# A hybrid attention and convolution layer: channel tiles reordered, the last two run by token halves, output weights split earlier

## The reference, cut to what matters

```
h    = rms_norm(x)
q, kv, gates, z_a, ch, cb, cc, cz = split(h @ w_in)
o_a  = (g0*compressed + g1*selected + g2*window attention) * silu(z_a)   # 8 heads x 64
u    = cc * ch
o_b  = cb * (conv3(u) + conv_b) * silu(cz)                               # 512 channels
out  = x + concat(o_a, o_b) @ w_out
```

## Time and profile before

| | us |
|---|---|
| median of three runs (lowest, highest) | 678.46 (677.49, 678.79) |
| the profiled execution's own time | 678.36 |
| its span, first to last instruction | 676.6 |
| TensorE busy | 654.6 (97%) |
| VectorE busy | 484.9 (72%) |
| ScalarE busy | 379.5 (56%) |
| GpSimd busy | 197.0 (29%) |

### The profile page before, as it was taken

The page is one execution under the profiler, slowest core; times in us unless marked ns, Lnnn a source line. Parts: engine busy times, 40 slices in busy tenths (PEclk is TensorE's granted clock), DMA queues, the critical chain, the costliest instruction groups (busy, mean ns, idle before and its releaser), DMA issues.

```text
span 676.6 us, 10300 instructions
## 1 busy us (share of the span) xinstructions
PE 654.6 (97%) x3513; PEld 550.9 (81%) x3513; DVE 484.9 (72%) x1151; ACT 379.5 (56%) x883; POOL 197.0 (29%) x216
## 2 busy tenths in 40 slices
PE   8999999999999999999989999899899999999998
PEld 5889998878887888888777888788678788887776
DVE  4945989984756555776687876878877768777753
ACT  6744458554435354466555674657875556655641
POOL 3423204523423232431222312123842221212120
PEclk9999999999999999999999999999999999999999
DMA  8423202211111111100101101011411001001111
GB/s 316 140 55 111 63 1 63 63 32 47 50 45 32 47 32 32 48 18 30 32 16 32 32 17 31 1 63 55 162 35 60 34 32 63 32 32 38 57 32 63
DMA packets 19636, 36.30 MB, mean 54 GB/s; under 512 B 2816, under 2 KB 4224, under 8 KB 19584
## 3 DMA queue, kind: packets, MB, share of 16 engines
q1 hardware_dynamic: 19440, 35.63, 16.9%
q10 hardware_dynamic: 144, 0.00, 0.0%
HBM read 31.43 MB, written 4.19 MB: 53 GB/s over the span
## 4 chain that ended last, share of the span: by engine, by line
PE 81%; DVE 10%; ACT 4%; issue 4%; DMA 1%; SPq 0%; POOL 0%; ACTq 0%; DVEq 0%
PE pf L1398 10%; PE pf L1399 9%; PE pf L1400 9%; PE tp L1691 7%; PE sc L1536 4%; PE pj L1400 4%; PE pj L1399 4%; PE pj L1398 4%; PE sc L1535 4%; PE po L1671 4%; PE po L1672 4%; PE sc L1398 3%; PE sc L1400 3%; PE sc L1399 3%; DVE ptl L1332 1%
## 5 line engine op out<-in xcount | busy, mean ns | idle before, releaser
L904 ACT CAST pth<-tp 128x512 fp32r<-128x512 f32 (+1 forms) x148 | 86.8, 586 | 119.8 <-PE tp L1691 118.6
L1310 DVE CUSTOM_DVE_ANT_0 sc<-sc,maskb 128x64 f32<-128x64 f32 (+8 forms) x192 | 103.2, 561 | 49.9 <-PE sc L1536 49.3
L1332 DVE TENSOR_TENSOR ptl<-tp,pth 128x512 fp32r<-128x512 f32 x132 | 91.1, 690 | 39.1 <-ACT pth L904 38.5
L627 POOL TENSOR_SCALAR qp<-qp,precip,gate 128x64 f32<-128x64 f32 x64 | 44.4, 694 | 175.4 <-DVE precip L1300 175.2
L1691 PE MATMUL tp<-cst,qp 128*128 128x128 f32 (+1 forms) x592 | 88.9, 272 | 2.4 <-issue 1.3
L1398 PE MATMUL pf<-hh,fh 128*128 128x512 f32 x200 | 80.6, 403 | 2.7 <-DVE mixc L1269 1.9
L1691 PEld LDWEIGHTS tp<-cst,qp 128*128 128x128 f32 (+1 forms) x592 | 68.8, 137 | 12.3 <-issue 3.4
L1399 PE MATMUL pf<-hl,fh 128*128 128x512 f32 x200 | 78.3, 392 | 0.0
L1400 PE MATMUL pf<-hh,fl 128*128 128x512 f32 x200 | 78.2, 391 | 0.0
L587 POOL TENSOR_TENSOR fl<-fraw,fh 128x512 fp32r<-128x512 f32 x36 | 48.7, 1354 | 92.7 <-ACT fh L753 92.7
L578 POOL TENSOR_TENSOR wl<-qp,wh 128x512 fp32r<-128x512 f32 (+1 forms) x33 | 49.3, 1519 | 88.8 <-ACT wh L667 85.2
(11 more groups left out here) (243 smaller groups left out, 1548.5 us busy)
## 6 DMA issues: line engine op xcount, KB each, us to landing
fraw<-in_wside SPq DMA_DIRECT2D x36, 256.0 KB, 2.6
qp<-in_wpack SPq DMA_DIRECT2D x28, 256.0 KB, 3.1
wor<-in_wout SPq DMA_DIRECT2D x16, 256.0 KB, 2.8
xo<-in_x SPq DMA_DIRECT2D x16, 256.0 KB, 2.8
out<-xo SPq DMA_DIRECT2D x16, 256.0 KB, 2.1
mixc<-in_xcm SPq DMA_DIRECT2D x4, 512.0 KB, 7.2
xlow<-in_xcm SPq DMA_DIRECT2D x3, 512.0 KB, 6.4
qp<-in_wpack SPq DMA_DIRECT2D x5, 224.0 KB, 2.6
```

The costliest lines, as they stand in the source:

```text
L904: nc.scalar.copy(pth[ptn % 2][0:r, :], tp[tpn % 2][0:r, :]).then_inc(pth_ready, 1)
L1310: return V.tensor_tensor_reduce(row, row, mask, -1.0, -NEG, ALU.add, ALU.min, most)
L1332: V.tensor_tensor(ptl[ptn % 2][:, :], tp[tpn % 2][:, :], pth[ptn % 2][:, :].bitcast(F32), ALU.subtract).then_inc(tp_read, 1)
```

## The change

1. In each group of four channel tiles cz now comes before cb. `cz_done` becomes `cz_used`: cb waits for the cz product, and cz, not cb, waits for the end of the convolution in its second half.
2. The last two tiles, cz3 and cb3, run by token halves: cz3 first half, cb3 first half, cz3 second half, cb3 second half. Their weights are loaded and split once for each half: `NHALF`, the count of loads of 256 KB, goes from 36 to 40.
3. The ACT operation that begins a convolution (L877) leaves the side work of step c (13, 29, 50, 74) and stands in step c+1 behind the exponentials and the first probability copy. On DVE the first convolution piece goes to the end of its step, and the others behind the side work of the first group.
4. The output weights are split in steps 81 to 84 (first eight pieces) and 87 to 90 (last eight) instead of 84 to 91. Four raw pieces of the first eight wait in `wor` or, for two of each four, in `xo`.
5. `xo`, `msh`, `msl` get memory of their own. The first `mixc` split goes from step 86 to 83, and the first `mixn` split from 88 to 85.
6. `SIDE` has no (0, 0) and no (1, 1) step any more. Three output halves (0, 1 and 13 of 0 to 15) run as four steps of (2, 0) each.
7. In the front, `keys_hi(0, 4, 1)` and `keys_lo(0, 4, 1)` go ahead of two z items; on DVE also ahead of the normalisation of the compressed key.

```diff
-    TILES += [("ch", t, 1816 + P * t), ("cc", t, 2840 + P * t), ("cb", t, 2328 + P * t), ("cz", t, 3352 + P * t)]
+    TILES += [("ch", t, 1816 + P * t), ("cc", t, 2840 + P * t), ("cz", t, 3352 + P * t), ("cb", t, 2328 + P * t)]
-NHALF = 2 * NTILES
+RUNS = [(n, hf) for n in range(NTILES - 2) for hf in range(2)]
+RUNS += [(n, hf) for hf in range(2) for n in (NTILES - 2, NTILES - 1)]
+SHARED = 2 * (NTILES - 2)
+NHALF = SHARED + 2 * (NF - SHARED)
+def first_load(f):
+    return 2 * (f // 2) if f < SHARED else 2 * f - SHARED
+def last_user(h):
+    return h // 2 * 2 + 1 if h < SHARED else (h + SHARED) // 2
+def load_source(h):
+    return h if h < SHARED else 2 * RUNS[last_user(h)][0] + h % 2
...
-SIDE = [(2, 2)] * 36 + [(2, 1), (2, 1), (2, 0)] * 17 + [(0, 0)] + [(1, 1)] * 8
-SIDE += [(2, 1), (2, 1), (2, 0)] * ((NS - len(SIDE)) // 3 + 2)
-SIDE = SIDE[:NS + 6] + [(4, 0)] * 4
+LONG = (NF, NF + 1, NX - 3)
+SIDE = [(2, 2)] * 36
+for x in range((SIDE_FIRST + sum(map(sum, SIDE))) // 8, NX - 2):
+    SIDE += [(2, 0)] * 4 if x in LONG else [(2, 1), (2, 1), (2, 0)]
+SIDE += [(4, 0)] * 4
...
-        if step_of(OUT_0 + 16 * m - (5 if m else 1)) == k:
+        if step_of(OUT_0 + 16 * m - (5 if m else 9)) == k:
...
-        if step_of(OUT_0 + 16 * m) == k:
+        if step_of(OUT_0 + 16 * m - (0 if m else 3)) == k:
...
-WOUT_STEP = step_of(OUT_0 - 9) + 1
+WOUT_STEPS = step_of(OUT_0 - 17) + 1, step_of(OUT_0 - 1) + 1
...
 # SP
-            for j in range(NK):
+            for j in range(NK + 4):
                 output_weights(j)
-            sp.wait_ge(f_done, NF)
+            sp.wait_ge(wol_ready, NK)
             for c in range(2):
                 residual(c)
...
 # ACT, front
             root(S_CK, 1, HD, ck_std)
+            keys_hi(0, 4, 1)
             item(E_Z, 1)
             item(E_Z, 2)
-            keys_hi(0, 4, 1)
             hidden(1)
...
 # ACT, side(f)
-                elif kind == "cc" and f % 2 == 1:
-                    bank_free(act, f - 1)
-                    bank_free(act, f)
-                    A(mixc[:, t, :], ub[:, 2:2 + SEQ], ACT.Identity, ...)
+            def convolve_first(t):
+                f = 2 * CONV_TILES[t] + 1
+                bank_free(act, f - 1)
+                bank_free(act, f)
+                A(mixc[:, t, :], ub[:, 2:2 + SEQ], ACT.Identity, ...)
...
 # ACT, step k, behind the exponentials and the first prob_hi
+                if k - 1 in CONV_STEPS:
+                    convolve_first(CONV_STEPS.index(k - 1))
...
-                    act.wait_ge(f_done, NF - 1 if j < NK else NF)
-                    nc.scalar.copy(woh[:, kt, cols], wor[j % 4][:, :]).then_inc(woh_ready, 1)
+                    act.wait_ge(f_done, NF - 2 if j < NK else NF)
+                    nc.scalar.copy(woh[:, kt, cols], weight_rows(j)[:, :]).then_inc(woh_ready, 1)
...
 # DVE, front
             V.tensor_reduce(stat[:, 0, S_CK:S_CK + 1], cksq[:, :], AX.X, ALU.add).then_inc(ck_sum, 1)
+            keys_lo(0, 4, 1)
             inv_std(S_CK, 1, HD, ck_std, 1)
...
             item(E_Z, 2)
-            keys_lo(0, 4, 1)
...
 # DVE, step k
-                for t, j in conv_pieces_at(k):
-                    convolve(t, j)
                 for f in side_ends(k, 0):
                     if f < NF:
                         side(f)
                 for c in out_ends(k, 0):
                     residual(c)
+                for t, j in conv_pieces_at(k):
+                    if j:
+                        convolve(t, j)
...
                 for c in out_ends(k, 1):
                     residual(c)
+                for t, j in conv_pieces_at(k):
+                    if j == 0:
+                        convolve(t, j)
```

More of the change, by code:

```diff
@@ L226, in mixn_half_at @@
     for m in range(LAST):
-        if step_of(OUT_0 + 16 * m) == k:
+        if step_of(OUT_0 + 16 * m - (0 if m else 3)) == k:
             return m
     return None
-CONV_STEPS = [step_of(16 * n + 15) for n in range(NTILES) if TILES[n][0] == "cc"]
+CONV_TILES = [n for n in range(NTILES) if TILES[n][0] == "cc"]
+CONV_STEPS = [step_of(16 * n + 15) for n in CONV_TILES]
 def conv_pieces_at(k):
@@ L241 @@
     for hf in range(2):
-        assert step_of(16 * TILES.index(("cb", t, 2328 + P * t)) + 8 * hf + 7) >= c + 2 + 2 * hf
-WOUT_STEP = step_of(OUT_0 - 9) + 1
+        assert step_of(8 * RUNS.index((TILES.index(("cz", t, 3352 + P * t)), hf)) + 7) >= c + 2 + 2 * hf
+WOUT_STEPS = step_of(OUT_0 - 17) + 1, step_of(OUT_0 - 1) + 1
 LAST_STEPS = (output_step(2 * LAST) + 6, output_step(2 * LAST + 1))
 def wout_at(k):
-    return [j for j in range(2 * NK) if WOUT_STEP + j // 2 == k]
+    return [NK * n + j for n in range(2) for j in range(NK) if WOUT_STEPS[n] + j // 2 == k]
 def wout_piece(j):
@@ L333, in hybrid_layer @@
                     fl[s] = sb(f"fl{s}", [P, 512], F32R, d)
[L334 to L339, removed]
+                with ExitStack() as f:
+                    fraw = [sb(f"fraw{s}", [P, 512], F32, f) for s in range(2)]
                 wor = [None, None] + [sb(f"wor{s}", [P, 512], F32, d) for s in (2, 3)]
@@ L348, in hybrid_layer @@
                 with ExitStack() as f:
-                    ub = sb("ub", [P, SEQ + 2], F32, f)
-                with ExitStack() as f:
                     wor[0], wor[1] = (sb(f"wor{s}", [P, 512], F32, f) for s in (0, 1))
+                ub = sb("ub", [P, SEQ + 2], F32, d)
+                xo = [sb(f"xo{s}", [P, 512], F32, d) for s in range(2)]
+                msh = sb("msh", [P, NK, P], F32R, d)
+                msl = sb("msl", [P, NK, P], F32R, d)
         with ExitStack() as c:
@@ L489, in half_free, with weight_rows @@
             else:
-                eng.wait_ge(f_done, h - 2)
+                eng.wait_ge(f_done, last_user(h - 3) + 1)
+        def weight_rows(j):
+            return xo[j % 4 - 2] if j < NK and j % 4 >= 2 else wor[j % 4]
         block = ctx.enter_context(nc.Block())
@@ L860, in side @@
             def side(f):
-                kind, t, _ = TILES[f // 2]
-                cols = slice(f % 2 * 512, (f % 2 + 1) * 512)
+                n, hf = RUNS[f]
+                kind, t, _ = TILES[n]
+                cols = slice(hf * 512, (hf + 1) * 512)
                 if kind in ("z", "cz"):
                     act.wait_ge(f_done, f + 1)
-                    if kind == "cz" and 2 * t + f % 2:
-                        act.wait_ge(cz_done, 2 * t + f % 2)
+                    if kind == "cz" and 2 * t + hf:
+                        act.wait_ge(cz_used, 2 * t + hf)
                     if kind == "z" and f >= 1:
@@ L1576, in channels @@
                 ins = three(side_bank(f), fh[h % 3][:, c], fl[h % 3][:, c], hh[:, k, s], hl[:, k, s], k == 0, k == NK - 1)
-                if hf == 1 and k == 3:
+                if k == 3 and last_user(h) == f:
                     ins.then_inc(half_used, 1)
```

49 lines of the change are left out of this document (24 added, 25 removed).

## The result

| | before | changed |
|---|---|---|
| median of four runs, us | 678.1 | 668.97 |
| lowest and highest | 677.49, 678.79 | 668.78, 669.98 |
| profiled execution, us | 678.36 | 669.98 |
| its span | 676.6 | 668.2 |

The ratio is 0.9868, with a 95% interval of 0.9851 to 0.9885: 1.3% faster. The predicted time was 670.8 us. The kernel before has one run more here than ahead of the change (677.73). The profiled execution of the changed kernel is the slowest of its four, so the two spans lie 8.4 us apart and the medians 9.1. Of the difference 0.7 us is found in the traces: from about 11 us on TensorE stands 0.7 us later in this execution, because its first operands came later; the last matmul of the hidden layer's first part starts at 149.17 us, before at 148.47.

A forecast was written before the change was run, and what follows sets the result against it. TensorE, 97% busy with unchanged matrix work, was the bound, so only its waits could go: 0.8 + 1.4 + 3.9 + 2.9 + 0.6 - 1.4 - 0.6 = 7.6 us, from 678.36 to 670.8. Likeliest range 669 to 673, wide range 667.0 to 677.0.

The forecast's parts named there:

- The front: Before the channels: the transposes' 1.38 us wait for DVE goes, the first channel split comes later; gain 0.8 us.
- L877 behind the exponentials: Waits behind ACT's first convolution operation go: 1.4 us in steps 14 and 30, 3.1 in steps 51 to 53 and 75.
- The bank after an attention output: Steps 54 and 78: a channel half's wait for DVE shortens by 0.74 us each, together 1.5.
- DVE's load as a discount: Steps 51 to 78: with DVE 96% busy some wait comes back, so of 4.6 us gain 3.9 is taken.
- Rival A: VectorE is the bound behind the waits: steps 51 to 78 gain 1.5, 86 to 94 gain 1.7; 675.0 us, chance 0.25.
- Steps 86 to 88 and 92 to 94: Waits of turn, scores and flush go in 86 to 88, gain 2.9 us; two like flushes in 92 to 94, 0.6.
- Four more splits: Extra channel splits in steps 78 to 82 slow DVE; with second cz operations and shifted residuals, loss 1.4 us.
- the weights split sooner: Output weights split from step 81: the 6.7 us buffer chain just fits two steps of some 3.6 us; taken at nothing.
- B: Rival: slower, as ACT waits for output weights in steps 81 to 84 and 87 to 90; 682.0 us, chance 0.07.
- The end: Steps 128 to 131: a second turn followed at once by its flush, afterwards also in step 131; loss 0.6 us.

The follow-up runs named there:

- keys_old: Changed kernel with the key copies of the front back in their old order on ACT and DVE: 669.94 us.
- conv_old: Changed kernel with ACT's first convolution operation back in the side work, ahead of the next exponentials; DVE's order stays new: 674.2 us.
- before_conv: Kernel before, with only ACT's first convolution operation moved behind the next step's exponentials and DVE's first piece to the end of its step: 672.61 us.
- pieces_first: Changed kernel with DVE's convolution pieces 1 to 3 back ahead of the side work of group 1: 670.11 us.
- swap_back: Changed kernel with cb ahead of cz again in every group of four, and their waits to match: 668.68 us.
- thin_steps: Changed kernel with the old step list: step 87 without a part, steps 88 to 95 with (1, 1): 671.64 us.
- shift_back: Changed kernel with the third output half of four (2, 0) steps being number 2 instead of 13: 669.37 us.

## Why the prediction was right, and where its terms were not

The forecast was 670.8 us, by its likeliest case 669 to 673; the median is 668.97, at that case's edge. The mechanism, waits that go while the matrix work stays, is shown. By its steps:

- **The front**, 0.8: 1.0 by medians in `keys_old`, 0.8 by the traces. It was right also in what is late next, the first channel split.
- **L877 behind the exponentials**, 1.4 and 3.1: shown, each wait with the size read. `conv_old` and `before_conv` give 5.2 us for it alone; beyond the 4.5 these are the delays of 0.21 and 0.17 us in steps 51 and 52, which the prediction did not list, and entries too small to list.
- **The bank after an attention output**, 1.5 listed: 1.3 less 0.4 given back, 0.9.
- **DVE's load as a discount**: of 4.6 listed for steps 51 to 78 the sum took 3.9, because DVE would be 96% busy and some wait would come back. The listed places gave 1.45 + 1.54 + 0.9 = 3.9: the size was right, and the 0.4 given back in steps 55 and 79 is of that kind, since it goes with the piece (`pieces_first`) or the second cz operation (`swap_back`) taken away. The stretch counted was 90% busy (six steps; the prediction says seven) with no wait over 0.27 us. The row's 4.9 holds 1.0 that was not listed: 0.4 in steps 51 and 52 with L877, and 0.5 in step 60 from the new order of cz and cb. Rival A's size, a loss of 3.1 of the 4.6, did not occur.
- **Steps 86 to 88 and 92 to 94**, 2.9 and 0.6: 3.2 and 0.5. The turn's wait is the order's doing (`swap_back` brings it back), those of the scores and of the flush the thin steps' (`thin_steps`).
- **Four more splits and "the weights split sooner"**: this step failed, 1.4 against 2.5, and the 1.4 was put on the wrong part. The four splits left next to no delay; one of the four met DVE. The moved output weights were "taken at nothing", as only the chain of buffers was costed; that chain did hold (no `woh` copy sat waiting for a landing, so B fell, and with two steps of 8.5 us in all, not the 7.2 of the prediction, it had more room). But the moved work cost step 84 nearly all of the 2.5 us, on two engines: ACT's copies of two pieces stood ahead of the exponentials of step 83 (1.0 us), and POOL's subtractions of `wol` lengthened DVE's scaling and product (0.36 and 1.08). The prediction had both mechanisms, copies ahead of exponentials in step 87 and POOL slowing DVE, and applied neither to the place where the moved work went.
- **The end**, 0.6: 1.5. Steps 127, 128 and 130 each have a second turn with nothing before its flush; the working looked at step 131 only, which has one turn and no such wait.
- **Not foreseen**: 2.0 us in steps 96 to 126, from alignment. Together with the end it made little (`shift_back`, 0.4 to 0.7 us), so the total came out right partly by luck: two misses of opposite sign, +2.0 and -2.0 (1.1 in step 84, 0.9 at the end), cancel. What is left, 1.5 us by medians, is mostly the 1.0 of steps 51, 52 and 60 that nobody listed. Which parts in which steps make or spare a wait from step 96 on was not taken apart further; that stays open.

The Trainium skill, "SBUF — State Buffer", section "Who interferes with whom", says that a DVE instruction with two inputs in SBUF contends with a GpSimd one that reads SBUF, and, of DVE's modes that use two ports, that whoever issues first has the shared pair for the whole instruction. The traces agree where DVE starts second: the product took 1.77 us beside a subtraction of 1.28 that began 0.07 us before it, 0.69 with POOL idle. L1301, which reads a bank of PSUM and one operand in SBUF, took 0.67 beside POOL's copies of `qd` and 0.69 without them. By that rule alone the forecast would have been 3.8 us later. A hit was about as long as that (0.9 and 1.1 us added, against up to 1.29), but of the four new subtractions one met such an instruction of DVE, and no delay of TensorE followed from it.

## What to carry to other kernels

An instruction that waits for another engine should stand behind everything in its list that is already ready: one of 1.24 us, four times, was worth 5.2 us here, mostly through delays a step or more later. When work is moved, cost what it meets at its new place on every engine, even if it is the same work: here copies ahead of exponentials on ScalarE, and GpSimd beside VectorE. List the waits that an edit should remove and look for each in the trace after; a busy share of 90% told neither where a wait would come back nor how long it would be.

## What was not expected of the hardware

- A one-element DVE product took 0.91 instead of 0.16 us, and one of 512 columns 1.77 instead of 0.69, beside a POOL subtraction of 1.28 to 1.29; the second delayed a flush by 1.1 us (1.24 against 0.16).
- The first operands arrive differently from execution to execution: the wait of one matmul of the start-up is 1.4 us in the changed kernel's profile and 0.2 in that of `thin_steps`, whose code is the same there; with the same front, the loop begins between 161.2 and 163.0 us. From the loop on, two traces of equal code agree within about 0.1 us a step, so sizes under 1 us can be read there and not from the medians.

```profile
PE xt L1466 <- ACT hh L701: 0.2, 1, 0.2
```

- A start is later than its idle entry says, by 0.16 us behind other matmuls, as predicted, and by 0.24 (0.50 against 0.74) at the flushes of the end: in the rows of the weight loads that gap is 0.74.
